# A token block on one core: tokens turned in groups of four tiles, and the modulation sums spread over the head steps

## The chip, the cores and the metric

The program runs on one core of one Trainium2 chip. The metric is the device time of one execution in microseconds (us); three runs are summed up by their median. On a core, TensorE (PE) multiplies matrices, VectorE (DVE), ScalarE (ACT) and GpSimd (POOL) work elementwise, and SyncE (SP) issues the transfers. Each engine works through its own list in order; they meet only at semaphores. Matrix products land in eight banks of 512 columns (PSUM), everything else is in SBUF.

## The reference

One layer of a diffusion backbone over 1024 latent tokens and 256 context tokens of width 1024. Six modulation rows (shift, scale and gate of two sub-layers) come from a SiLU of the condition times a 1024x6144 matrix. Rows 0 and 1 shape the input of the token mixer; row 2 gates its output; rows 3 and 4 shape the input of the feed-forward, row 5 gates that.

```python
def modulate(x, gain, shift, scale):
    return rms_norm(x, gain) * (1 + scale) + shift
...
        mx = jnp.split((sc @ w_mod[l] + b_mod[l])[:, None, :], N_MOD, axis=-1)
        px = split_proj(modulate(x, pre_mix_g[l], mx[0], mx[1]) @ w_in[l])
        pc = split_proj(modulate(xc, pre_mix_g[l], mc[0], mc[1]) @ w_in[l])
        oc, s_f, s_b = hgrn_bidir(*hgrn_inputs(pc, lb_f, lb_b), zero_state, zero_state)
        ox, _, _ = hgrn_bidir(*hgrn_inputs(px, lb_f, lb_b), s_f, s_b)
        mix_x = mixer_output(ox, px, rows, w_out[l], hgrn_onorm_g[l], conv_dw_w[l],
                             conv_dw_b[l], conv_ln_g[l], conv_ln_b[l])
        x = x + mx[2] * rms_norm(mix_x, post_mix_g[l])
        hx = swiglu(modulate(x, pre_ffn_g[l], mx[3], mx[4]), ffn_w_gate[l], ffn_w_up[l], ffn_w_down[l])
        x = x + mx[5] * rms_norm(hx, post_ffn_g[l])
```

The token mixer has four heads. Each head has seven projections (`b` and `a` for the convolution, `ff` and `fb` for the two forget gates, `q`, `g`, `v`), a two-way gated recurrence, and a convolution with 31 taps on 128 channels.

## The kernel before

**Front.** SP loads row 1 of the modulation matrix (eight tiles `mraw`), two token tiles with two weight tiles, then row 0, and then the other tokens. TensorE multiplies the rows by the condition (`mod_step`), ScalarE copies the product (`mod_rows`) and TensorE turns it into columns; VectorE adds the bias (`mod_take`). The ten token tiles (eight latent, then two of context) go one by one: ScalarE sums squares (`x_rms`), VectorE scales the tile (`norm_x`), TensorE transposes it in eight blocks (`turn_x`, line 618), VectorE applies gain and shift to each 128 columns (line 1387), ScalarE rounds to a high part (line 947), and GpSimd subtracts for the low part (`lo_part`, line 1238). Every large product is made of three products of such parts, so a tile can be used only once both parts stand.

**Head steps.** Step 0 runs the first head's projections. Steps 1 to 3 are one loop: each runs the projections of a head and between them the recurrence of the head before. A step has 20 units (`UNITS`): unit 0 and 1 `b`, 2 and 3 `a`, 4 to 6 `ff`, 7 to 9 `fb`, 10 and 11 `q`, 12 and 13 `g`, 14, 15 and 17 `v`; 16, 18 and 19 turn `v`. `PE_STEPS` fixes which uses of the recurrence follow a unit: the levels 0 to 7 after units 0 to 7, state products after 9 to 11, the output ("o") after 12, which needs the states of `rec_states`. Three banks turn over for units, five for uses. VectorE's order is `dve_body`: per unit `take`, `rec_step`, and as many convolution taps as `TAPS_AFTER` says. `rec_start` (lines 1433 to 1443) opens a step, before anything else.

**The other four rows.** Rows 2 to 5 of the modulation matrix are summed on VectorE in step 0, 32 chunks of 128x1024 (`mod_chunk`, lines 1369 and 1372) into four rows of `macc`. After step 0, TensorE sums them over partitions (`mod_sum`, 8 products each against a column of ones), VectorE takes them (`mod_take`, line 1350), and the loop waits for all four.

**Weights.** Three slots (`ringa`, `ringb`, `ringc`) hold weight tiles; tile p+1 of a slot is loaded when the last unit of the tile before it is done, ScalarE copies the high part (`head_hi`, line 935), GpSimd makes the low one. SP's queue is in order, so a load behind a waiting one waits too.

## Time and profile before

| | us |
|---|---|
| median of 3 runs | 1452.11 (1450.2 to 1452.63) |
| the profiled execution | 1452.88 |
| its span, first to last instruction | 1451.1 |
| TensorE busy | 1375.9 (95%) |
| VectorE, ScalarE, GpSimd busy | 778.6, 377.3, 324.2 |
| mean granted TensorE clock | 0.970 |

A row of the timeline gives start, duration, engine, line, operation and names, and in brackets how long the engine stood idle before, and what released it. A product of two 32-bit operands is two rows for TensorE, so "x16" of such a kind is eight products. A matmul's shown end is modelled and overlaps the next one by about 0.17 us.

### The profile page before, as it was taken

The numbers are of one execution on the slowest core, as the hardware profiler recorded it, in microseconds if no ns is written. First come the engines' busy times: TensorE is split into PE (matmuls) and PEld (weight loads), VectorE is DVE, ScalarE is ACT, GpSimd is POOL, SyncE is SP. The second block draws the span as 40 slices with busy tenths as digits, with TensorE's granted clock in tenths as the row PEclk, the third lists the DMA queues.
The fourth block names the chain that finished last, engine by engine and source line by source line (L and its number), as shares of the span: only waits on it lengthen the run. The fifth ranks groups of instructions, "written<-read, shape, count | busy, mean of one in ns | idle before, by whom it ended". The sixth has DMA issues, their size and how long they took to land. (4 is left out here: it accounts for less than half of the span.)

```text
span 1451.1 us, 17647 instructions
## 1 busy us (share of the span) xinstructions
PE 1375.9 (95%) x6725; PEld 1148.5 (79%) x6725; DVE 778.6 (54%) x1020; ACT 377.3 (26%) x562; POOL 324.2 (22%) x135
## 2 busy tenths in 40 slices
PE   6699899999999997898989999999999999999998
PEld 1588788888888886687768888888888888888876
DVE  2899969769778879818721313232232313232227
ACT  3521222132232234616631121111111121111112
POOL 1522111021111124503524122122122122122110
PEclk9699799999999998999999999999999999999999
DMA  9384110110010010004321111101101111101132
GB/s 370 155 284 165 29 30 16 30 44 28 29 43 29 14 68 34 1 25 164 136 68 29 50 39 58 58 31 57 57 29 58 49 39 57 58 30 57 51 124 116
DMA packets 94704, 101.94 MB, mean 70 GB/s; under 512 B 3118, under 2 KB 77091, under 8 KB 94658
## 3 DMA queue, kind: packets, MB, share of 16 engines
q1 hardware_dynamic: 94658, 101.32, 20.5%
q8 instruction: 29, 0.48, 0.1%
q14 instruction: 17, 0.14, 0.0%
HBM read 92.92 MB, written 8.39 MB: 70 GB/s over the span
## 5 line engine op out<-in xcount | busy, mean ns | idle before, releaser
L1238 POOL TENSOR_TENSOR slot<-slotraw,slot 128x1024 fp32r<-128x1024 f32 x66 | 160.5, 2442 | 522.2 <-ACT slot L1174 313.8
L561 PE MATMUL bank<-h2Ta,slot 128*128 128x512 f32 x1056 | 247.5, 394 | 5.2 <-POOL slot L1238 4.9
L561 PE MATMUL bank<-slot,mid 128*128 128x512 f32 x1056 | 242.9, 391 | 1.8 <-POOL slot L1238 1.8
L561 PEld LDWEIGHTS bank<-h2Ta,slot 128*128 128x128 f32 x1056 | 200.4, 190 | 47.8 <-POOL slot L1238 5.3
L561 PEld LDWEIGHTS bank<-slot,mid 128*128 128x128 f32 x1056 | 199.3, 189 | 43.8 <-POOL slot L1238 2.2
L561 PE MATMUL bank<-cathi,slot 128*128 128x512 f32 x704 | 220.2, 389 | 0.0
L1419 DVE SCALAR_TENSOR_TENSOR cat<-conv_u,taps,cat 128x784 f32 (+29 forms) x120 | 150.6, 1255 | 12.6 <-DVE cat L1419 6.2
L561 PEld LDWEIGHTS bank<-cathi,slot 128*128 128x128 f32 x704 | 132.1, 188 | 27.7 <-issue 0.3
L561 PE MATMUL bank<-hT,ringb 128*128 128x512 f32 (+1 forms) x672 | 149.1, 378 | 0.4 <-DVE cat L1402 0.4
L1694 DVE TENSOR_TENSOR mid<-bank,sgm 128x512 f32<-128x512 f32 x44 | 30.4, 692 | 221.7 <-ACT sgm L1189 221.7
L1719 DVE TENSOR_TENSOR arena<-bank,arena 128x512 f32<-128x512 f32 x144 | 99.5, 691 | 90.0 <-PE bank L561 89.5
L561 PE MATMUL bank<-catlo,slot 128*128 128x512 f32 x352 | 136.9, 389 | 0.0
L561 PEld LDWEIGHTS bank<-hT,ringb 128*128 128x128 f32 x672 | 118.6, 188 | 22.4 <-DVE cat L1402 0.8
L1697 DVE TENSOR_TENSOR mid<-bank,mid 128x512 f32<-128x512 f32 x44 | 30.4, 692 | 170.6 <-PE bank L561 170.5
L561 PE MATMUL bank<-hT,ringa 128*128 128x512 f32 (+1 forms) x480 | 109.1, 386 | 7.5 <-DVE mod L1350 5.5
L561 PEld LDWEIGHTS bank<-hT,ringa 128*128 128x128 f32 x480 | 87.0, 198 | 24.1 <-issue 5.5
L561 PE MATMUL bank<-hT,ringc 128*128 128x512 f32 (+1 forms) x480 | 102.8, 371 | 0.0
L561 PEld LDWEIGHTS bank<-hT,ringc 128*128 128x128 f32 x480 | 83.0, 189 | 14.3
L561 PE MATMUL bank<-wo,cathi 128*128 128x512 f32 x256 | 83.3, 407 | 5.3 <-POOL catlo L1238 3.7
L1189 ACT ACTIVATE sgm<-bank 128x512 f32<-128x512 f32 x44 | 26.1, 595 | 234.8 <-PE bank L561 234.8
L561 PEld LDWEIGHTS bank<-catlo,slot 128*128 128x128 f32 x352 | 66.1, 188 | 13.7
L561 PE MATMUL bank<-Q,KC 128*128 128x128 f32 x448 | 62.7, 297 | 10.1 <-DVE Q L1474 7.0
(171 smaller groups left out, 1516.7 us busy)
## 6 DMA issues: line engine op xcount, KB each, us to landing
mraw<-in_w_mod SPq DMA_DIRECT2D x48, 512.0 KB, 7.0
slotraw<-in_ffn_w_gate SPq DMA_DIRECT2D x22, 512.0 KB, 3.7
slotraw<-in_ffn_w_up SPq DMA_DIRECT2D x22, 512.0 KB, 3.8
slotraw<-in_ffn_w_down SPq DMA_DIRECT2D x22, 512.0 KB, 3.9
ringinb<-in_w_in SPq DMA_DIRECT2D x12, 512.0 KB, 3.6
xst<-in_x SPq DMA_DIRECT2D x8, 512.0 KB, 13.7
ringina<-in_w_in SPq DMA_DIRECT2D x8, 512.0 KB, 4.7
ringinc<-in_w_in SPq DMA_DIRECT2D x8, 512.0 KB, 4.7
```

What stands on the lines that cost most here:

```text
L561: return pe.matmul(o, l, r, start=start, stop=stop, skip_group_check=True)
L1189: act.activation(sgm[:, p, :], bank[gu_at(n, pos)[2]][:], ACT.Sigmoid).then_inc(gu_sig, 1)
L1238: return pool.tensor_tensor(lo, full, hi.bitcast(F32), ALU.subtract)
L1419: conv_last[0] = step(dve.scalar_tensor_tensor(out, src, w, out, ALU.mult, ALU.add))
L1694: dve.tensor_tensor(mid32[:, p, :], bank[b0][:], sgm[:, p, :], ALU.mult).then_inc(gu_part, 1)
L1697: dve.tensor_tensor(mid32[:, p, :], bank[b0 + 1][:], mid32[:, p, :], ALU.mult).then_inc(gu_free, 1)
L1719: ins = dve.tensor_tensor(y_half(t, hf), b[:], y_half(t, hf), ALU.add)
```

## The change

Four things are changed together.

First, tokens are turned in three groups (four latent tiles, four latent tiles, two context tiles). Instead of scaling a tile and transposing it, VectorE scales the identity (`diag`), and TensorE multiplies each 128x128 block of tokens by that diagonal, so that a block comes out turned and normalised; four tiles fill one bank, and one affine step covers 512 columns (256 for the context). ScalarE makes the high part straight from the bank (`part_hi`), VectorE the full one (`part_full`), and low parts alternate between VectorE (`part_lo`) and GpSimd. Five of the 24 turns stand between the fourth and the fifth chunk of the second modulation row.

Second, the second and third unit change places: unit 1 is now the first half of `a`, unit 2 the second half of `b`. Step 0 runs units 0 and 1 after group 0 alone.

Third, step 0 sums only rows 2 and 3 (16 chunks). Rows 4 and 5 are summed in the second and third steps, those with s = 1 and s = 2, in eight chunks each (`late_chunk`) through one buffer. The column sums (`mod_sum`) stand after unit 13 of step 0 (row 2) and ahead of unit 19 of steps 0, 1 and 2 (rows 3, 4, 5); VectorE takes each at the start of the next step (`late_take`), and unit 1 waits for it.

Fourth, the loop runs over s = 1 and 2, and step 3 is written out behind it.

```diff
...
+GROUPS = [range(0, 4), range(4, 8), range(8, 10)]
+XBANK = [0, 1, 2, 4, 6, 3, 5, 7] + [3 + r % 5 for r in range(16)]
...
+UNITS[1], UNITS[2] = UNITS[2], UNITS[1]
...
-CHUNKS_AFTER = [4, 4, 4, 4, 4, 4, 4, 4]
-TAPS_FIRST = [0, 0, 0, 0, 0, 0, 0, 0, 3, 3, 3, 3, 3, 3, 2, 2, 2, 2, 2, 2]
+CHUNKS_FIRST = [0, 2, 2, 2, 2, 2, 2, 2, 2]
+CHUNK_LATE = [3, 5, 7, 9, 11, 13, 15, 17]
+TAPS_FIRST = [0, 0, 0, 1, 1, 1, 1, 1, 1, 3, 3, 3, 3, 2, 2, 2, 2, 2, 2, 0]
...
+        macc = sb("macc", [P, DM], offset=spot["K"])
         vT = sb("vT", [P, 2, BANK], offset=RAW0 + RAW * 2 * DM * 4)
+        diag = sb("diag", [P, 8, P], offset=RAW0 + RAW * 2 * DM * 4)
...
+        def x_part(i):
+            g, k = i // KT, i % KT
+            t0, n = TORD[GROUPS[g][0]] * P, len(GROUPS[g]) * P
+            a = 1 if g == 2 else 0
+            return (slice(t0, t0 + n), bank[XBANK[i]][:, 0:n], xfull[:, i % 4, 0:n],
+                    gain[:, k, a:a + 1], mod[:, 0, k, a:a + 1])
...
+            def load_late(s, k):
+                sp.wait_ge(mod_used, s * KT + (KT + k))
+                sp.dma_start(mraw[:, 7, :].rearrange("p (o n) -> p o n", o=1),
...
             load_mod(0)
-            for t in range(2):
+            for t in range(4):
                 load_x(t)
-                load_tile(0, t)
+            load_tile(0, 0)
             load_mod(1)
...
+            load_tile(0, 1)
+            for t in range(4, NT):
...
             load_tile(0, 2)
-            for c in range(4 * KT):
-                if c in (12, 18, 24):
-                    load_tile(0, c // 6 + 1)
+            for c in range(2 * KT):
+                if c in (10, 12):
+                    load_tile(0, c // 2 - 2)
                 load_chunk(c)
+            load_tile(0, 5)
+            load_tile(1, 0)
             load_tile(0, 6)
-            with sp.Fori(1, HEADS) as s:
-                for p in range(NTILE):
-                    load_tile(s, p)
+            with sp.Fori(1, HEADS - 1) as s:
+                load_tile(s, 1)
+                load_tile(s, 2)
+                load_late(s, 0)
+                load_tile(s, 3)
+                load_tile(s, 4)
+                load_late(s, 1)
+                load_tile(s, 5)
+                for k in range(2, 5):
+                    load_late(s, k)
+                load_tile(s, 6)
+                load_tile(s + 1, 0)
+                for k in range(5, KT):
+                    load_late(s, k)
+            for p in range(1, NTILE):
+                load_tile(HEADS - 1, p)
...
+            def mod_sum(s, src, out):
+                pe.wait_ge(mod_used, s * KT + 2 * KT)
                 for j in range(KT):
-                    ins = mm(bank[LBASE + n - 2][:, j:j + 1], macc[:, n - 2, j * P:(j + 1) * P], ones[:, 0:1], True, True)
+                    ins = mm(out[:, j:j + 1], src[:, j * P:(j + 1) * P], ones[:, 0:1], True, True)
                 ins.then_inc(mod_turned, 1)
...
+            def turn_x(i):
+                g, k = i // KT, i % KT
+                if k == 0:
+                    pe.wait_ge(xn_ready, GROUPS[g][-1] + 1)
+                if i == 5:
+                    pe.wait_ge(mod_done, 2)
+                earlier = [j for j in range(i) if XBANK[j] == XBANK[i]]
+                if earlier:
+                    pe.wait_ge(x_hi, earlier[-1] + 1)
+                    pe.wait_ge(x_full, earlier[-1] + 1)
+                for c, t in enumerate(GROUPS[g]):
+                    ins = mm(bank[XBANK[i]][:, c * P:(c + 1) * P], xst[:, t, k * P:(k + 1) * P], diag[:, t % 8, :],
+                             True, True)
+                ins.then_inc(xp_full, 1)
...
+            for k in range(KT + 1):
+                mod_step(1, k)
+                if k == 3:
+                    for i in range(5):
+                        turn_x(i)
...
+                if u == NUNIT - 1 and row:
+                    mod_sum(s, cat[:, 3], b[:, 2 * P:])
...
+                        if first(s) and u in (0, 2, 4):
+                            i = u // 2 * KT + k
+                            pe.wait_ge(lo_pool if i % 2 else lo_dve, i // 2 + 1)
...
+            for i in range(5, KT):
+                turn_x(i)
             project(0, 0)
-            for t in range(7, NT):
-                turn_x(t)
-            for u in range(1, NUNIT):
-                if u == 1 or u == 4:
-                    pe.wait_ge(h_lo, 8 if u == 1 else NT)
+            project(0, 1)
+            for i in range(KT, 3 * KT):
+                turn_x(i)
+            for u in range(2, NUNIT):
                 project(0, u)
...
+                if u == 13:
+                    mod_sum(-1, macc[:], bank[LBASE])
...
+            def pe_step(s, row):
                 for u in range(NUNIT):
-                    project(s, u)
+                    if u == (NUNIT - 1) % GRING:
+                        pe.wait_ge(mod_done, s + 3)
+                    project(s, u, row)
                     for i in PE_STEPS[u]:
                         use(s - 1, i)
+            pe.wait_ge(mod_done, 3)
+            with pe.Fori(1, HEADS - 1) as s:
+                pe_step(s, True)
+            pe_step(HEADS - 1, False)
...
+            def part_hi(i):
+                sl, src, _, scale, shift = x_part(i)
+                act.wait_ge(mod_done, 2)
+                act.wait_ge(xp_full, i + 1)
+                act.activation(hT[:, 0, i % KT, sl], src, ACT.Identity, scale=scale, bias=shift).then_inc(x_hi, 1)
...
+            for t in range(4):
                 x_rms(t)
...
+            head_hi(0, 0)
...
+            for i in range(KT):
+                part_hi(i)
+            for t in range(4, 8):
+                if t == 5:
+                    head_hi(0, 1)
+                x_rms(t)
+            for i in range(KT, 2 * KT):
+                part_hi(i)
+                if i % KT in (3, 5):
+                    x_rms(7 + i % KT // 2)
+            for i in range(2 * KT, 3 * KT):
+                part_hi(i)
...
+            for g in range(3):
+                if g < 2:
+                    head_lo(0, g)
+                for i in range(g * KT + 1, (g + 1) * KT, 2):
+                    sl, _, full, _, _ = x_part(i)
+                    pool.wait_ge(x_full, i + 1)
+                    lo_part(hT[:, 1, i % KT, sl], full, hT[:, 0, i % KT, sl]).then_inc(lo_pool, 1)
...
-                dve.tensor_scalar(xst[:, t, :], xst[:, t, :], rr[:, 0, t:t + 1], None, ALU.mult).then_inc(xn_ready, 1)
+                if t >= 8:
+                    dve.wait_ge(xp_full, KT)
+                dve.tensor_scalar(diag[:, t % 8, :], ident[:], rr[:, 0, t:t + 1], None, ALU.mult).then_inc(xn_ready, 1)
...
+            def late_take(s):
+                dve.wait_ge(mod_turned, s + 3)
+                dve.wait_ge(gemm_act, s * N_GACT + N_GACT)
+                b = bank[(NUNIT - 1) % GRING][:, 2 * P:2 * P + KT]
+                dve.tensor_tensor(mod[:, bass.ds(s + 2, 1), :, 0:1], b.rearrange("p (o k a) -> p o k a", o=1, a=1),
+                                  vec[:, bass.ds(s * KT + (R_BM + 2 * KT), KT)].rearrange("p (o k a) -> p o k a", o=1, a=1),
+                                  ALU.add).then_inc(mod_done, 1)
...
+            def late_gains():
+                dve.wait_ge(mod_done, 6)
+                step(dve.scalar_tensor_tensor(gain2[:], mod[:, 4, :, 0], 1.0, vec[:, R_PREF:R_PREF + KT], ALU.add, ALU.mult))
+                step(dve.tensor_tensor(gate[:, 1], mod[:, 5, :, 0], vec[:, R_POSTF:R_POSTF + KT], ALU.mult))
+            def late_chunk(s, k):
+                dve.wait_ge(late_in, s * (16 * KT) + 16 * (k + 1 - KT))
+                src, w, acc = mraw[:, 7, :], silc[:, k, 0:1], cat[:, 3]
+                if k == 0:
+                    ins = dve.tensor_scalar(acc, src, w, None, ALU.mult)
+                else:
+                    dve.wait_ge(mod_used, s * KT + (KT + k))
+                    ins = dve.scalar_tensor_tensor(acc, src, w, acc, ALU.mult, ALU.add)
+                ins.then_inc(mod_used, 1)
...
-                src, w, acc = mraw[:, CHUNK_AT[c % NCH], :], silc[:, k, 0:1], macc[:, n, :]
+                src, w, acc = mraw[:, CHUNK_AT[c % NCH], :], silc[:, k, 0:1], cat[:, 3] if n else macc[:]
...
+            def part_full(i):
+                _, src, full, scale, shift = x_part(i)
+                dve.wait_ge(x_hi, i + 1)
+                if i >= 4 and i % 2:
+                    dve.wait_ge(lo_pool, (i - 4) // 2 + 1)
+                elif i >= 4:
+                    dve.wait_ge(lo_dve, (i - 4) // 2 + 1)
+                dve.tensor_scalar(full, src, scale, shift, ALU.mult, ALU.add).then_inc(x_full, 1)
+            def part_lo(i):
+                sl, _, full, _, _ = x_part(i)
+                dve.wait_ge(x_full, i + 1)
+                dve.tensor_tensor(hT[:, 1, i % KT, sl], full, hT[:, 0, i % KT, sl].bitcast(F32),
+                                  ALU.subtract).then_inc(lo_dve, 1)
...
+            for t in GROUPS[0]:
+                norm_x(t)
             mod_take(1)
...
+            for g in range(3):
+                if g:
+                    for t in GROUPS[g]:
+                        norm_x(t)
+                for i in range(g * KT, (g + 1) * KT, 2):
+                    part_full(i)
+                    part_full(i + 1)
+                    part_lo(i)
...
                     if rec:
                         rec_step(s - 1, u, 1)
+                        if u == 0:
+                            late_take(s)
+                        if more and u in CHUNK_LATE:
+                            late_chunk(s, CHUNK_LATE.index(u))
                     else:
-                        for c in taps_after(CHUNKS_AFTER, u):
+                        for c in taps_after(CHUNKS_FIRST, u):
                             mod_chunk(c)
+                        if u == 15:
+                            mod_take(2)
...
+            dve_body(HEADS - 1, True, TAPS_AFTER, False)
...
-                if u == 1:
+                if u == 0:
+                    late_gains()
...
```

On TensorE at the front, what stands from the first modulation row to the fifth unit, before:

```order
L561 MATMUL bank<-mraw,silc 32x512 x16
L561 MATMUL bank<-sel,mrow 128x2 x8
L561 MATMUL bank<-mraw,silc 32x512 x16
L561 MATMUL bank<-sel,mrow 128x2 x8
L618 MATMUL bank<-ident,xst 128x128 x56
L561 MATMUL bank<-hT,ringa 128x512 x24
L618 MATMUL bank<-ident,xst 128x128 x24
L561 MATMUL bank<-hT,ringa 128x512 x24
L561 MATMUL bank<-hT,ringb 128x512 x48
```

And in the changed program:

```order
L597 MATMUL bank<-mraw,silc 32x512 x8
L597 MATMUL bank<-diag,xst 128x128 x20
L597 MATMUL bank<-mraw,silc 32x512 x8
L597 MATMUL bank<-sel,mrow 128x2 x8
L597 MATMUL bank<-diag,xst 128x128 x12
L597 MATMUL bank<-hT,ringa 128x512 x24
L597 MATMUL bank<-hT,ringb 128x512 x24
L597 MATMUL bank<-diag,xst 128x128 x48
L597 MATMUL bank<-hT,ringa 128x512 x24
L597 MATMUL bank<-hT,ringb 128x512 x24
```

The turns now stand in three pieces (20 between the row's chunks, 12 ahead of unit 0, 48 behind unit 1), and two units run before the last 48.

On VectorE, the last taps of the loop's body before (`cat<-conv_u` is a tap; ISA and REGISTER_ALU rows are the sequencer's own):

```order
L1419 SCALAR_TENSOR_TENSOR cat<-conv_u,taps,cat 128x16x50
L359 REGISTER_ALU
L1419 ISA
L1419 SCALAR_TENSOR_TENSOR cat<-conv_u,taps,cat 128x16x49
L359 REGISTER_ALU
L1572 REGISTER_ALU
L1572 COMPARE_AND_BRANCH
```

And in the changed program, where `mraw` rows are late chunks:

```order
L1521 SCALAR_TENSOR_TENSOR cat<-conv_u,taps,cat 128x16x50
L1445 REGISTER_ALU
L1450 REGISTER_ALU
L1451 SCALAR_TENSOR_TENSOR cat<-mraw,silc,cat 128x1024
L365 REGISTER_ALU
L1521 ISA
L1521 SCALAR_TENSOR_TENSOR cat<-conv_u,taps,cat 128x16x49
L1450 REGISTER_ALU
L1451 SCALAR_TENSOR_TENSOR cat<-mraw,silc,cat 128x1024
L365 REGISTER_ALU
L1678 REGISTER_ALU
L1678 COMPARE_AND_BRANCH
```

The seventh and the eighth late chunk have one tap between them, and nothing behind them but the loop's branch.

On SP, the end of the loop's body before, the loads of the last two tiles:

```order
L468 DMA ringinc<-in_w_in 128x8x128
L465 REGISTER_ALU
L468 ISA
L468 DMA ringinb<-in_w_in 128x8x128
L484 REGISTER_ALU
```

And in the changed program:

```order
L482 DMA ringinb<-in_w_in 128x8x128
L481 ISA
L482 ISA
L482 DMA ringina<-in_w_in 128x8x128
L487 REGISTER_ALU
L488 ISA
L488 DMA mraw<-in_w_mod 128x1024
L487 REGISTER_ALU
L488 ISA
L488 DMA mraw<-in_w_mod 128x1024
L487 REGISTER_ALU
L488 ISA
```

The next step's first weight tile is now asked for in this body, and the last late chunks behind it; the next step's second tile comes behind these.

## Rows read from the trace of the kernel before

**Rows 1.** The page: busy time, share and instructions of each engine.

```profile
PE 1375.9 (95%) x6725; PEld 1148.5 (79%) x6725; DVE 778.6 (54%) x1020; ACT 377.3 (26%) x562; POOL 324.2 (22%) x135
```

**Rows 2.** Windows: us; busy (count) PE PEld DVE ACT POOL; granted clock, DMA share, GB/s.

```profile
45.00:56.00 11.00, 6.67 (x30) 5.47 (x29) 10.89 (x34) 7.94 (x14) 7.82 (x4) 0.50 0.46 189
63.00:66.00 3.00, 2.74 (x21) 2.29 (x19) 1.53 (x5) 0.20 (x1) 1.32 (x1) 1.00 0.00 0
```

**Rows 3.** TensorE's waits in 38 to 72 and 152 to 190: total, times, longest.

```profile
PE bank L618 <- DVE xst L1339: 10.1, 6, 2.3
...
PE bank L561 <- DVE mod L1350: 5.5, 1, 5.5
```

**Rows 4.** Timeline, the second modulation row: start, us, engine, line, names.

```profile
24.10 7.30 PE L561 MATMUL bank<-mraw,silc 128*32 128x512 f32 x24 [3.05 <-DMA mraw<-in_w_mod]
...
32.87 1.05 PE L561 MATMUL bank<-mraw,silc 128*32 128x512 f32 x4 [0.20 <-DMA mraw<-in_w_mod]
...
36.60 0.17 DVE L1347 TENSOR_TENSOR mod<-bank,vec 128x16 f32<-128x16 f32 x1 [8.74 <-PE bank L561]
```

**Rows 5.** Timeline, one token tile and the two units of 56 and 70.

```profile
54.69 2.64 DVE L1387 TENSOR_SCALAR xfull<-bank,gain,mod 128x128 f32<-128x128 f32 x8
...
56.45 7.54 PE L561 MATMUL bank<-hT,ringa 128*128 128x512 f32 x24
...
70.68 7.30 PE L561 MATMUL bank<-hT,ringa 128*128 128x512 f32 x24 [1.56 <-POOL hT L1238]
...
77.82 11.04 PE L561 MATMUL bank<-hT,ringb 128*128 128x512 f32 x48
78.02 0.60 ACT L968 ACTIVATE cat<-bank 128x512 f32<-128x512 f32 x1 [1.63 <-PE bank L561]
```

**Rows 6.** Timeline, the end of step 0 and the start of step 1.

```profile
144.04 5.79 PE L561 MATMUL bank<-hT,ringb 128*128 128x512 f32 x24 [0.42 <-DVE cat L1402]
...
153.96 11.99 PE L561 MATMUL bank<-ones,macc 128*128 128x1 f32 x64
...
171.40 8.09 PE L561 MATMUL bank<-hT,ringa 128*128 128x512 f32 x24 [5.45 <-DVE mod L1350]
171.49 1.80 DVE L1433 TENSOR_SCALAR K<-F,lb 128x1280 f32<-128x1280 f32 x2 [0.23 <-issue]
...
178.85 1.49 DVE L1443 TENSOR_TENSOR T<-F 128x1280 f32<-128x1280 f32 x1
...
179.33 3.73 PE L561 MATMUL bank<-qraw,K 128*128 128x128 f32 x32
```

**Rows 7.** Timeline of VectorE and GpSimd inside step 1; TensorE's waits for the states.

```profile
213.01 2.40 POOL L1238 TENSOR_TENSOR ringa<-ringina,ringa 128x1024 fp32r<-128x1024 f32 x1 [17.17 <-ACT ringa L935]
...
213.09 3.48 DVE L1474 TENSOR_TENSOR Q<-Q,T 128x512 f32<-128x512 f32 x2 [0.40 <-PE bank L561]
...
232.26 3.38 DVE L1474 TENSOR_TENSOR Q<-Q,T 128x512 f32<-128x512 f32 x2 [1.13 <-PE bank L561]
...
264.65 0.49 PE L561 MATMUL bank<-AT,V 128*128 128x128 f32 x2 [1.71 <-DVE S L1506]
```

**Rows 8.** Timeline, the end of step 1 and the start of step 2.

```profile
275.59 1.84 PE L561 MATMUL bank<-ones,AT 128*128 128x1 f32 x16
277.29 5.75 PE L561 MATMUL bank<-hT,ringb 128*128 128x512 f32 x24
...
285.94 4.67 DVE L1419 SCALAR_TENSOR_TENSOR cat<-conv_u,taps,cat 128x832 f32 x4
```

**Rows 9.** Timeline of TensorE: equal products behind two of its waits.

```profile
555.20 3.70 PE L561 MATMUL bank<-Q,KC 128*128 128x128 f32 x16 [4.87 <-DVE Q L1474]
588.36 2.78 PE L561 MATMUL bank<-Q,KC 128*128 128x128 f32 x16 [2.44 <-ACT KC L987]
```

**Rows 10.** The tile mraw: chunk adds, min/median/max ns; loads to landing.

```profile
L1372 DVE SCALAR_TENSOR_TENSOR macc<-mraw,silc,macc x28: 1279/1284/3299, 74.7 to 124.3; 128x1024 f32<-128x1024 f32 x28
...
DMA to landing us min/median/max: 3.5/7.0/11.6
```

More of the change, by code:

```diff
@@ L105 @@
     PE_STEPS[_at].append(_i)
-CHUNKS_AFTER = [4, 4, 4, 4, 4, 4, 4, 4]
-TAPS_FIRST = [0, 0, 0, 0, 0, 0, 0, 0, 3, 3, 3, 3, 3, 3, 2, 2, 2, 2, 2, 2]
+CHUNKS_FIRST = [0, 2, 2, 2, 2, 2, 2, 2, 2]
+CHUNK_LATE = [3, 5, 7, 9, 11, 13, 15, 17]
+TAPS_FIRST = [0, 0, 0, 1, 1, 1, 1, 1, 1, 3, 3, 3, 3, 2, 2, 2, 2, 2, 2, 0]
 TAPS_AFTER = [0, 0, 0, 0, 1, 1, 1, 1, 3, 2, 4, 4, 3, 3, 3, 3, 0, 1, 0, 0]
 assert sum(TAPS_FIRST) == sum(TAPS_AFTER) == TAPS - 1
-assert sum(CHUNKS_AFTER) == 4 * KT
+assert sum(CHUNKS_FIRST) == 2 * KT and len(CHUNK_LATE) == KT
 WO_ORDER = [0, 1, 2, 4, 5, 6, 7, 3]
@@ L398, in kernel_program @@
         MODS = [1, 0, 2, 3, 4, 5]
-        CHUNK_AT = [1, 2, 3, 5, 6, 7]
+        CHUNK_AT = [1, 2, 5, 6, 7]
         NCH = len(CHUNK_AT)
@@ L626, in wait_bank, with project @@
                 pe.wait_ge(act_sem if who == "act" else dve_sem, s * n + ((1 - ago) * n + k + 1))
-            def project(s, u):
+            def project(s, u, row=True):
                 p, kind, n = UNITS[u]
@@ L1349, in mod_take @@
                 else:
-                    dve.tensor_tensor(mod[:, m, :, 0], bank[LBASE + n - 2][:, 0:KT],
+                    dve.tensor_tensor(mod[:, m, :, 0], bank[LBASE][:, 0:KT],
                                       vec[:, R_BM + m * KT:R_BM + (m + 1) * KT], ALU.add).then_inc(mod_done, 1)
                 dve.wait_ge(mod_done, n + 1)
-                one = mod[:, m, :, 0]
                 if m == 1:
@@ L1356, in mod_take @@
                                                   ALU.add, ALU.mult))
-                elif m == 4:
-                    step(dve.scalar_tensor_tensor(gain2[:], one, 1.0, vec[:, R_PREF:R_PREF + KT], ALU.add, ALU.mult))
-                elif m in (2, 5):
-                    g, r0 = (0, R_POSTM) if m == 2 else (1, R_POSTF)
-                    step(dve.tensor_tensor(gate[:, g], one, vec[:, r0:r0 + KT], ALU.mult))
+                elif m == 2:
+                    step(dve.tensor_tensor(gate[:, 0], mod[:, m, :, 0], vec[:, R_POSTM:R_POSTM + KT], ALU.mult))
+            def late_take(s):
[18 more added lines that the diff above has]
+                ins.then_inc(mod_used, 1)
             def mod_chunk(c):
@@ L1373, in mod_chunk @@
                 ins.then_inc(mod_used, 1)
-            norm_x(0)
-            norm_x(1)
+            def part_full(i):
[11 more added lines that the diff above has]
+                                  ALU.subtract).then_inc(lo_dve, 1)
             mod_take(0)
+            for t in GROUPS[0]:
+                norm_x(t)
             mod_take(1)
             step.wait()
-            for t in range(NT):
-                a = 1 if TORD[t] < CT else 0
-                for k in range(KT):
-                    if k % 4 == 0:
-                        dve.wait_ge(xp_full, 2 * t + k // 4 + 1)
-                    if k == 0 and t >= 2:
-                        dve.wait_ge(h_lo, t - 1)
-                    ins = dve.tensor_scalar(xfull[:, t % 2, k, :],
-                                            bank[LBASE + (2 * t + k // 4) % 4][:, (k % 4) * P:(k % 4 + 1) * P],
-                                            gain[:, k, a:a + 1], mod[:, 0, k, a:a + 1], ALU.mult, ALU.add)
-                    if k % 4 == 3:
-                        ins.then_inc(xp_free, 1)
-                if t + 2 < NT:
-                    norm_x(t + 2)
+            for g in range(3):
[6 more added lines that the diff above has]
+                    part_lo(i)
             def take(s, u):
@@ L1548, in rec_step, with dve_body @@
                     rec_out(h, u)
-            def dve_body(s, rec, taps):
+            def dve_body(s, rec, taps, more):
                 for u in range(NUNIT):
```

64 lines of the change are left out of this document (14 added, 50 removed).

## The prediction

> **What bounds the kernel now.** I read the busy times first. TensorE works 1375.9 of 1451.1 us [rows 1], so a change pays only where it takes products away or an idle stretch of TensorE. Next I read TensorE's waits by releaser, and two stretches stand out. While tokens are turned it waits six times for VectorE to scale a tile, 10.1 us in all; before step 1 it waits once, 5.5 us, for the modulation rows [rows 3]. The timeline of the first stretch shows VectorE as the pacemaker: a tile's eight affine steps take 2.64 us [rows 5], the scaling comes on top, and TensorE runs at a granted clock of 0.50 [rows 2], its half level. At the end of step 0 the 64 rows of column sums run 11.99 us from 153.96, then comes the wait, then step 1 starts at 171.40 with a slow unit [rows 6]. Last I read the waits inside the loop, since work moves there: short ones, such as 1.71 us ahead of the output products [rows 7].
>
> The profiled execution is 1452.88: the span 1451.1 and 1.78 around it. It stands 0.77 above the median of 1452.11, so what I forecast for the profile is lowered by 0.7 or so. A measurement can't tell less than 0.2%, 2.9 us: "same" is 1449.2 to 1455.0.
>
> **Term 1, the front.** Row 0 of the modulation is complete at 36.77 (36.60 and 0.17) [rows 4]. Its eight chunks arrive in order, 32.87 - 24.10 = 8.77 over seven, 1.25 each [rows 4]. Two more token tiles and one weight tile less stand ahead of it on SP: one tile net, +1.25. Between its fourth and fifth chunk come 20 turn products. No row shows a product with a diagonal; by form the nearest are the column sums, 16 rows or eight products in 1.70 (277.29 - 275.59), 0.2125 each at the full clock [rows 8], and 32 products in 11.99, 0.375 each at the half [rows 6]. The 20 cost 4.25 or 7.5; I take 4.25, as they stand in a dense stretch. The last four chunks lie in memory by then and cost 0.53 to 1.05 each instead of 1.25. So M, both rows done, moves from 36.77 to about 40.4 (bounds 39.5 and 43.7).
>
> From M on VectorE makes group 0. No row shows an affine step of 512 columns from a bank; eight of 128 take 2.64 [rows 5], and one 1024-wide add 1.28 [rows 10]. I take 0.7 for 512 columns and as much for the subtraction: a pair of blocks is two affine steps and one low part, 2.05, and four pairs 8.2. With ScalarE's first high part (0.60 for 512 columns, [rows 5]) and GpSimd's last low part (half of 2.40 [rows 7], 1.2) unit 0 ends at about M + 10.5. Unit 1 wants its own weight tile, whose high part ScalarE makes behind eight activations, the table load and a sum of squares, and GpSimd the low one in 2.4: it starts near M + 12.2 and ends at M + 17.8. Then come group 1's 32 turns (6.8), VectorE's second 8.2 and the diagonals, group 2's 16 turns (3.4 to 5.1), and unit 2 starts at about M + 35.3 = 75.7. In the kernel before unit 1 starts at 70.68 [rows 5].
>
> **Term 2, the rest of step 0.** From 70.68 to the end of the last turned block, 153.96 + 0.15, are 83.43 us; unit 1 itself takes 7.14 of them (77.82 - 70.68) [rows 5, 6]. Left are 76.3, and two column sums of 1.70 are added: 79.7. Step 1 then starts at 155.4 to 155.8, against 171.40: 15.8 earlier. The gap of half-clock sums and waiting also goes, and with it the slow unit behind it: 179.33 - 171.40 = 7.93 against about 5.56 for a unit at the full clock (5.75 with the overlap, [rows 8]), 2.4. Term 2 with term 1 is -18.2. Both ends: -21 if VectorE's affine steps are at 0.6 and the tail of group 2 hides, -14 if the 20 turns go at the half clock and VectorE pays for every pair separately. What was the column sums' cover before, 16 chunks on VectorE beside step 0, goes to the loop.
>
> **Term 3, unit 1 of step 1.** It now waits for `late_take`, which stands behind `rec_start` and the first `rec_step` on VectorE. `rec_start` takes 8.85 us (171.49 to 178.85 and 1.49) [rows 6]. When it can begin depends on what VectorE has left of step 0. Behind unit 13, which ends near 144.04 [rows 6], 12 taps are left at 1.17 (4.67 for four, [rows 8]) and up to 1.28 each, 14 to 15.4, and TensorE has 10.1 + 1.7 + 1.7 of work to the end of the step: VectorE is about 1 us late. GpSimd's low parts hold it up too: two VectorE instructions of 512 columns took 3.48 beside a GpSimd row that began 0.08 earlier, where one of 1024 takes 1.28 [rows 7, 10]; I add one such 2.1. Step start + 12.1 against TensorE's arrival after unit 0 and level 0, 5.56 + 3.5 = 9.04: a wait of 3.1, and 0.7 of clock behind it, +3.8. Bounds 0 (VectorE on time, not blocked) and +6 (two blocks). Steps 2 and 3 have the same wait in their list, but there the taps end earlier, and I charge none.
>
> **Term 4, steps 1 and 2 with the late chunks.** Three costs each.
> The sum ahead of unit 19: 1.70 [rows 8].
> The output products: TensorE waits 1.71 for the states [rows 7]. Chunks after units 3, 5, 7, 9 stand ahead of that on VectorE: one of about 0.75 and three of 1.28 with some blocking, 4.8. The pauses of VectorE that can take it up are 0.40 and 1.13 and the like [rows 7], some 3.3 by then. Bounds of the growth 1.1 (a pause I haven't seen takes more) and 4.8 (none does); by the pauses 1.5 would come out, but they lie ahead of the third chunk for the most part, and I take 2.8.
> The last chunk: all eight go through one buffer, and chunk 7 is asked for when chunk 6 has been added, after unit 15. A load of `mraw` takes 3.5 us at least, 7.0 in the median [rows 10]; those were issued in crowds, one alone is nearer the 3.5. Add 1.28 for the chunk and one tap. Between unit 15's take and unit 19's sum TensorE has units 16 to 18 and three turned pieces, and VectorE reaches chunk 6 itself late, 15 slots down its list. I get a wait of 3.2; bounds 0 and 6.5 (the median landing).
> A clock that falls in these waits: behind a wait of 4.87 sixteen products took 3.70, behind 2.44 2.78 [rows 9], against about 1.87 (32 in 3.73, [rows 6]); behind a wait of 1.71 two ran in 0.49 at full pace [rows 7]. So a wait of 3 to 4 costs some 1.2 more in all (0 to 3).
> Together 1.70 + 2.8 + 3.2 + 1.2 = +8.9 for a step, +17.8 for both; bounds +5.6 and +32, of which the far one wants every wait at its worst.
>
> **Term 5, small things.** Step 3 is written out and its output wait may lose 1.71 [rows 7], as VectorE's list there is free of register instructions: -1.7 (bound 0). `late_gains`, two rows of 0.17 like the one in [rows 4], stand where TensorE waits 4.87 for VectorE [rows 9]: +0.35. Units 1 and 2 change places: the same 48 products; VectorE's work on them moves by one unit and was waited for by nobody: 0 (bounds -1 and +1).
>
> Sum: -18.2 + 3.8 + 17.8 - 1.7 + 0.35 = +2.05, 1454.9 for the profiled execution, 1454.2 for the median.
>
> **Rivals.**
> A, the forecast: what the front gives back the loop takes. Its own range is 1450.5 to 1458, from each wait moved by a third of its bounds.
> R1, slower: the load-to-add chain of the single buffer decides. If a load takes 5 us or more under the weights' traffic, chunks 5 to 7 slide and the sum of unit 19 waits 6.5 instead of 3.2, twice, and the clock falls behind it: 2 x 3.3 + 1 = +7.6, 1461.8. It decides from a landing of about 4.5 us on. For it: the median 7.0 [rows 10]. Against it: the transfers in the loop are few.
> R2, faster: VectorE has more slack than I see, being 54% busy [rows 1]. Then unit 1 of step 1 doesn't wait (-3.8) and the output wait doesn't grow by more than 1.1 (2 x -1.7): 1447.0. Against it: rows such as 3.48 instead of 1.28 beside GpSimd [rows 7], and that the waits for states are already there.
> R3, the clock in the front rises: now TensorE has products that are no transposes. Unit 0 then takes 5.75 and not 7.54 [rows 5, 8], and the last four chunks go at 0.53: -2.7, 1451.5. For it: 0.50 while transposes are waited for [rows 2]. Against it: 63 to 66 was at 1.00 with transposes running, though right behind a unit, and 45 to 56 had TensorE idle for 4 of 11 us, which explains the half level as well [rows 2].
> The Trainium skill, "TensorE: Matmul & The Clock Gate", section "Part 4: PE-mode transpose", states that the full clock doesn't engage for transposes, which don't count as busy in the same way. By that rule R3 is what would come; the trace doesn't settle it, since its fast transposes could have inherited the clock of the unit ahead of them.
> R4, slower: SP's queue is in order, and weight tiles now stand behind chunk loads: tile 3 of step 0 behind chunk 9, and the next step's tile 1 behind the eighth late chunk, which is asked for only after chunk 6 is added. If that is later than the slot came free, unit 2 of the next step starts on its weights late, by about 2.5 us twice: +5, 1459. Against it: tile 1 has the whole of unit 0 and unit 1, 15 us, before it is wanted.
>
> **How the numbers follow.** A 0.47, of which 0.04 is faster, 0.31 same, 0.12 slower by more than 0.2%; R1 0.21 (slower); R2 0.18 (faster); R3 0.09 (same); R4 0.05 (slower). Faster 0.22, same 0.40, slower 0.38. The time is A's, 1454.2. From 1447 to 1461 the range takes in A, R3, R4, half of R1 and more than half of R2; what is left out is under 2 in 10.
>
> **What would show it in the profile after.** M at 40.4 and the 20 turns at 0.2125 each; unit 0's end at 51, unit 1 at full speed, unit 2 at 75.7; the granted clock of 30 to 60, which tells R3; step 1's start at 155.6; TensorE's wait for `late_take` before step 1's unit 1 (3.1, none in steps 2 and 3); the output waits of steps 1 and 2 (4.5, from 1.71) and of step 3 (0); the wait ahead of the sum before unit 19 (3.2) with the landing time of the late loads, which tells R1; and no wait of ScalarE's copy for the tile of unit 2, which tells R4. I am wrong if step 1 starts later than 159, if the sum's wait is near 0, or if TensorE shows no new wait in the loop.

## The result and the profile after

The changed kernel takes 1460.87 us (1459.87 to 1461.79) against 1451.87: ratio 1.0063, 95% interval 1.0046 to 1.0081. It is slower by 9.0 us where 1454.2 was forecast, at the far edge of the stated range (1447 to 1461). The profiled execution is 1461.46, its span 1459.7.

The timeline of TensorE up to unit 2, and between its rows VectorE's take of the second modulation row (start, us, engine, line, names):

```profile
30.84 4.88 PE L597 MATMUL bank<-diag,xst 128*128 128x128 f32 x40
...
40.31 0.17 DVE L1416 TENSOR_TENSOR mod<-bank,vec 128x16 f32<-128x16 f32 x1 [13.85 <-PE bank L597]
...
53.20 5.73 PE L597 MATMUL bank<-hT,ringb 128*128 128x512 f32 x24 [1.34 <-POOL ringb L1304]
...
71.93 5.56 PE L597 MATMUL bank<-diag,xst 128*128 128x128 f32 x32 [5.84 <-DVE diag L1408]
...
77.24 3.02 PE L597 MATMUL bank<-hT,ringa 128*128 128x512 f32 x12
```

M, the time at which both modulation rows are done, is 40.48 (forecast 40.4), unit 1 starts at 53.20 (52.6), unit 2 at 77.24 (75.7). In the kernel before, two units and all turns were done by 77.82 [rows 5], here by 77.24: turning in groups is worth 0.6 us by then, although VectorE no longer paces each tile. One wait of 5.84 for the last diagonals took the place of most of the six (10.1 in all).

The end of step 0, and TensorE's two long waits of step 1:

```profile
155.92 5.74 PE L597 MATMUL bank<-hT,ringa 128*128 128x512 f32 x24
161.50 3.73 PE L597 MATMUL bank<-qraw,K 128*128 128x128 f32 x32
167.75 7.31 PE L597 MATMUL bank<-hT,ringb 128*128 128x512 f32 x24 [2.52 <-DVE mod L1433]
...
253.45 0.80 PE L597 MATMUL bank<-AT,V 128*128 128x128 f32 x2 [3.32 <-DVE S L1608]
...
287.21 3.58 PE L597 MATMUL bank<-ones,cat 128*128 128x1 f32 x16 [2.95 <-DVE cat L1451]
290.65 0.67 PE L688 MATMUL bank<-ident,vT 128*128 128x128 f32 x2
290.97 7.13 PE L597 MATMUL bank<-hT,ringa 128*128 128x512 f32 x24
```

Step 1 starts at 155.92 instead of 171.40 [rows 6]: 15.5 us are won. Then they are lost. Behind each wait the reader sees products that should be faster: sixteen column-sum rows in 3.58 that take 1.84 elsewhere [rows 8], a first unit in 7.13 instead of 5.73. The windows around them (us; busy of PE, PEld, DVE, ACT, POOL; granted clock, DMA share, GB/s) show why:

```profile
253.00:257.00 4.00, 3.55 (x19) 3.55 (x20) 3.51 (x6) 0.00 (x0) 0.00 (x0) 0.57 0.19 35
257.00:260.00 3.00, 3.00 (x29) 3.00 (x28) 2.30 (x2) 0.00 (x0) 0.00 (x0) 1.00 0.33 128
...
287.00:291.00 4.00, 3.79 (x19) 3.79 (x19) 0.28 (x2) 0.00 (x0) 0.00 (x0) 0.52 0.92 300
```

Behind these waits of about 3 us TensorE runs at its half level (1.2 GHz): for some 3 us behind the waits for the states (253.4 to 256.5) and for nearly 7 behind those ahead of the sum (287.2 to 294.0). From level 0 to level 0 (the products of `qraw` and `K`) step 1 is 136.44 us long and step 2 132.76, where the kernel before has 121.00 and 120.97.

VectorE at the end of step 1:

```profile
280.58 1.28 DVE L1451 SCALAR_TENSOR_TENSOR cat<-mraw,silc,cat 128x1024 f32<-128x1024 f32 x1
281.78 1.03 DVE L1521 SCALAR_TENSOR_TENSOR cat<-conv_u,taps,cat 128x784 f32 x1
285.88 1.28 DVE L1451 SCALAR_TENSOR_TENSOR cat<-mraw,silc,cat 128x1024 f32<-128x1024 f32 x1 [3.07 <-DMA mraw<-in_w_mod]
290.88 1.80 DVE L1535 TENSOR_SCALAR K<-F,lb 128x1280 f32<-128x1280 f32 x2 [3.72 <-issue]
```

The last chunk waits for its load, which is asked for at 282.0, when the chunk before it is added, and lands 3.7 later. Then come 3.72 us in which VectorE waits for nothing that the profile shows. They lie at the loop's jump back: in the trace VectorE's row of the branch (line 1678) ends at 286.21, and its next row of any kind, at the head of the loop, begins at 290.60. Before step 3, which follows without a jump, rec_start begins at 419.81, right behind the chunk of 418.60 to 419.88.

The tail lost 1.1 us:

```profile
552.45 2.31 DVE L1440 SCALAR_TENSOR_TENSOR gain<-mod,vec 128x8 f32<-128x8 f32 x1
...
558.34 5.58 DVE L1576 TENSOR_TENSOR Q<-Q,F 128x512 f32<-128x512 f32 x2
...
564.06 3.49 PE L597 MATMUL bank<-Q,KC 128*128 128x128 f32 x16 [6.27 <-DVE Q L1576]
```

The wait of [rows 9] grew from 4.87 to 6.27. An instruction of `late_gains` that writes eight numbers per partition took 2.31 us beside GpSimd's low parts, not 0.17; but the next ones took longer too (the two of `Q` 5.58, in the kernel before 4.62). Whether the wait hangs on `late_gains`, 'take first' tells.

### The profile page after: what moved, and what is told of

Read it like the earlier page. It is cut to its first block and busy times, and to the rows that moved or that the text cites. A ratio compares the mean times of both kernels' runs of the same rounds, so it can differ in the third digit from the quotient of the medians.

```text
span 1459.7 us, 17675 instructions
## 1 busy us (share of the span) xinstructions
PE 1379.7 (95%) x6805; PEld 1156.9 (79%) x6805; DVE 763.3 (52%) x976; ACT 381.9 (26%) x576; POOL 318.5 (22%) x137
## 5 line engine op out<-in xcount | busy, mean ns | idle before, releaser
L1521 DVE SCALAR_TENSOR_TENSOR cat<-conv_u,taps,cat 128x784 f32<-128x784 f32 (+29 forms) x120 | 149.9, 1249 | 8.4 <-DVE cat L1521 4.1
L597 PE MATMUL bank<-Q,KC 128*128 128x128 f32 x448 | 62.5, 297 | 12.9 <-DVE Q L1576 8.6
```

The lines of the kernel that those rows point to most:

```text
L597: return pe.matmul(o, l, r, start=start, stop=stop, skip_group_check=True)
L1521: conv_last[0] = step(dve.scalar_tensor_tensor(out, src, w, out, ALU.mult, ALU.add))
```

## Experiments

Times are medians; the kernel before, run beside them, was 1451.1, 1451.5 and 1451.6.

**What the additions cost.** The loads and `late_chunk` are left out, so rows 4 and 5 are not summed; the column sums and takes stay.

```diff
...
-                        if more and u in CHUNK_LATE:
-                            late_chunk(s, CHUNK_LATE.index(u))
...
```

> Left out: the loads and the additions of modulation rows 4 and 5 (the column sums, the takes and all other instructions stay, on a row that is already there). Theory 'clock': the waits ahead of unit 19 and their slow products go (12.1), and ahead of the output products 2 x 1.6 of waiting and 2 x 1.42 of slow products: 1460.9 - 18.1 = 1442.8. Rival 'the loop costs for another reason' (units changed in order, the written-out third step, the sums themselves): it stays above 1452. The two column sums of 1.70 are in either number.

1441.50, ratio 0.9935 (0.9921 to 0.9948). The wait for the states is back to 1.69 with no slow product behind it, and the sum runs without a wait:

```profile
251.07 0.49 PE L591 MATMUL bank<-AT,V 128*128 128x128 f32 x2 [1.69 <-DVE S L1602]
...
280.30 1.84 PE L591 MATMUL bank<-ones,cat 128*128 128x1 f32 x16
```

So 19.4 us hang on sixteen additions and their loads. The additions take about as long on VectorE (14 of 1.28 and two of 0.73), an engine that is busy for half the time. The rival falls: neither the changed order of units nor the sums themselves cost them.

**The clock apart from the waits.**

```diff
...
+                    if not first(s):
+                        fill(b[:, 3 * P:4 * P], 14, P)
                     mod_sum(s, cat[:, 3], b[:, 2 * P:])
...
```

and the same (14 spare products) ahead of the wait for the states.

> In steps 1 and 2 TensorE runs 14 spare products of 128 columns (about 3.0 us) ahead of the column sum's wait, and 14 ahead of the wait for the states; nothing reads them. The waits' length is filled, not removed. Theory 'clock': the granted clock stays up, and only the slow products behind the waits go: 1.74 + 1.40 + 1.43 + 1.74 ahead of and behind the step's end, 2 x 1.42 at the output products, 9.1 in all, so 1451.8. Rival 'waits alone': 1460.9, or 1 more where the filler overshoots.

1458.80, 2.1 less than the changed kernel, not 9.1. The two steps tell different things. Step 2, level 0 to level 0, is 127.38 instead of 132.76: 5.4 less for waits that are about as long as before, only full of spare products. The granted clock of 419 to 427 is 1.00. Of the 5.4, 0.45 is unit 1's wait for the take, which is gone too; the rest agrees with the 4.8 of slow products counted in that step. So there the clock accounts for some four tenths of the 11.8 us that the step had grown by. In step 1 a stall of TensorE at the jump took the gain:

```profile
286.19 1.84 PE L597 MATMUL bank<-ones,cat 128*128 128x1 f32 x16
287.90 0.41 PE L694 MATMUL bank<-ident,vT 128*128 128x128 f32 x2
292.27 7.33 PE L597 MATMUL bank<-hT,ringa 128*128 128x512 f32 x24 [3.96 <-issue]
```

TensorE's row of the branch lasts 5.65 us here and 0.23 in the changed kernel, and the unit behind the stall is slow again.

**The sum's place.**

```diff
...
-                if u == NUNIT - 1 and row:
-                    mod_sum(s, cat[:, 3], b[:, 2 * P:])
...
+                    if u == 0:
+                        pe.wait_ge(gemm_act, s * N_GACT + N_GACT)
+                        mod_sum(s - 1, cat[:, 3], bank[(NUNIT - 1) % GRING][:, 2 * P:])
```

> The column sums of rows 3, 4 and 5 stand behind unit 0 of the next step instead of ahead of unit 19; all else as in the changed kernel (1460.9). Theory 'clock': each of the two waits ahead of unit 19 (2.95 and 2.86 us) costs its own length and, by a granted clock that falls in it, slow products behind it (the sum 3.58 and 3.27 instead of 1.84, the first unit of the next step 6.97 and 7.31 to its successor instead of 5.57). Both go: 2.95 + 2.86 + 1.74 + 1.43 + 1.40 + 1.74 = 12.1, so 1448.8. Rival 'waits alone' (the slow products are slow for a reason of their own, such as one-column products): only 5.8 goes, 1455.1, and the first units of steps 2 and 3 stay near 7.1. Rival 'the wait moves': the last chunk is late at the new place too, 1457 or more.

1457.89 (1455.35 to 1460.64), ratio 1.0045. The first units of steps 2 and 3 are fast again (5.72), so the slow products are not slow of themselves. But the time is that of the rival 'the wait moves':

```profile
293.85 3.84 PE L597 MATMUL bank<-qraw,K 128*128 128x128 f32 x32 [0.96 <-DVE K L1536]
301.15 5.72 PE L597 MATMUL bank<-hT,ringb 128*128 128x512 f32 x24 [3.46 <-DVE mod L1434]
```

Unit 1 of step 2 starts at 301.15, only 1.0 earlier than in the changed kernel (302.12). A second chain ends there: last chunk, VectorE's stall of 4.08 at the jump, rec_start, take. TensorE's wait and its slow products in front had run beside it. In step 3, with no jump, unit 1 is 4.5 earlier (429.68 against 434.19).

The row at 301.15 shows something else: its unit stands behind a wait of 3.46 and still takes 5.72, at a granted clock of 1.00 from 301 to 307. The length of a wait alone doesn't decide whether the clock falls behind it.

**The take, and the gains of the tail.** `late_take` stands ahead of rec_start, `late_gains` after the last swish.

> VectorE takes each late row before rec_start instead of behind it, and late_gains stands where VectorE is idle in the tail. Theory 'clock': in step 1 the wait of unit 1 (2.52) and the slow unit behind it (7.15 instead of 5.55 to its successor, 1.6) go, in step 2 0.45, and in the tail VectorE's rows before the products no longer contain the 2.31 of late_gains, 1.1: 1460.9 - 5.7 = 1455.2. Rival 'waits alone': 1456.8. Rival 'VectorE is late with rec_start anyway': level 0 or 1 waits instead, 1460.

1454.39, ratio 1.0013 (1.0004 to 1.0022): 6.5 less, where 5.7 was expected. Unit 1 of step 1 starts at 165.76, with no wait, and takes 5.70. But 1.1 of the 5.7 was to come from the tail, and it didn't; step 2 gave 2.3 instead of 0.45. There the products behind the wait for the states, as long as in step 1 (3.31 and 3.34), kept the full clock, and the output took 5.38 instead of 7.01. The windows behind the wait in step 1 and in step 2:

```profile
250.00:254.00 4.00, 4.00 (x22) 4.00 (x23) 3.75 (x4) 0.00 (x0) 0.00 (x0) 0.58 0.32 92
382.00:387.00 5.00, 5.00 (x45) 5.00 (x46) 4.49 (x5) 0.00 (x0) 0.00 (x0) 1.00 0.34 105
```

So part of the good agreement is luck. The tail's wait stays at 6.2 without `late_gains` in front, so the 2.31 was not its cause:

```profile
548.90 3.65 DVE L1568 TENSOR_TENSOR K<-K,F 128x1280 f32<-128x1280 f32 x1 [2.23 <-ACT KC L1052]
552.47 5.58 DVE L1576 TENSOR_TENSOR Q<-Q,F 128x512 f32<-128x512 f32 x2
```

VectorE now idles 2.23 for ScalarE where it was blocked before, and the products with `Q` are as slow beside GpSimd. How these lists meet GpSimd's decides the wait (4.0 in 'all moved', 6.2 here, 5.9 to 6.2 in the changed kernels written out, 3.9 in the kernel before written out), and no run here sorts it out.

**The chunks' places**, on top of the moved sum.

```diff
...
-CHUNK_LATE = [3, 5, 7, 9, 11, 13, 15, 17]
+CHUNK_LATE = [0, 1, 2, 11, 12, 13, 14, 15]
...
```

> As 'sum behind unit 0' (1457.9, its profiled execution 1456.0), and the eight late chunks stand after units 0, 1, 2, 11, 12, 13, 14, 15 instead of 3, 5, ..., 17, with the loads moved ahead on SP to match. Theory 'VectorE's list sets both ends' (the chunks ahead of the states; at the step's end the last chunk behind its load, then 4.08 us at the loop's branch, then rec_start, then the take): the output waits fall from 3.3 to about 1.7 and their slow products (1.42) go, twice, 6.0; and with the last chunk over before unit 16, the wait of unit 1 in steps 2 and 3 (3.46 and 0.6) goes for the most part, 3: 1457.9 - 9 = 1449. Rival 'the chunks only move their cost' (VectorE's early pauses are not there, and levels 1 to 3 wait instead): 1456 to 1460.

1449.55, ratio 0.9984 (0.9976 to 0.9993). The two waits for the states are 3.4 together instead of 6.6; three chunks at the start of a step fit into pauses in which VectorE waited for TensorE. The time is the expected 1449, but the waits at the start of steps 2 and 3 did not go for the most part: level 0 waits 2.57, unit 1 1.83 and 1.93. The jump costs more here: 5.93 us lie between VectorE's row of the branch and its next row, although the last chunk is over before.

**All of it**: the moved sum, the chunks' places, the take in the middle of rec_start, the gains.

> As 'early_chunks', and the take of a late row stands in the middle of rec_start (ahead of its products with Q), and late_gains stands where VectorE is idle in the tail. Theory: on top of 'early_chunks' step 1's wait of 2.5 and its slow unit (1.6) go, and 1.1 in the tail: 1449 - 5.2 = 1444, faster than the kernel before (1451.1). Rival 'a waiting take in rec_start delays level 0 or 1': 1448.

1439.29, ratio 0.9927 (0.9912 to 0.9943): faster than both kernels, and 4.7 under what was expected. Of these, 2.3 are the tail's wait, 3.95 instead of 6.26. What is left at the start of step 2 is the stall at the jump, 5.23 here, and again slow products (5.18 instead of 3.82) behind a short wait:

```profile
284.66 1.80 DVE L1536 TENSOR_SCALAR K<-F,lb 128x1280 f32<-128x1280 f32 x2 [5.23 <-issue]
...
286.51 5.18 PE L597 MATMUL bank<-qraw,K 128*128 128x128 f32 x32 [1.33 <-DVE K L1536]
```

**The loop's own cost.** Five kernels have the steps written out on TensorE, VectorE, ScalarE and SyncE (the kernel before on TensorE, VectorE and SyncE alone):

```diff
...
-            with dve.Fori(1, HEADS - 1) as s:
+            for s in range(1, HEADS - 1):
...
```

> As 'sum behind unit 0' (1457.9), with steps 1 and 2 written out on TensorE, VectorE, ScalarE and SyncE instead of a loop. Theory 'branch': VectorE's 4.08 us of idling between the last chunk and rec_start is the jump back; without it rec_start of step 2 starts near 287.5 and unit 1's wait of 3.46 falls to about 0.3: 1454.5. Rival 'issue is something else' (fetching goes on at the same pace without a branch): 1457.9, with the same idle time.

1445.01 (1439.8 to 1452.8), ratio 0.9963 (0.9950 to 0.9977): 12.9 less than its loop form, not 3.4. VectorE's row of rec_start follows the last chunk at once:

```profile
279.51 1.28 DVE L1452 SCALAR_TENSOR_TENSOR cat<-mraw,silc,cat 128x1024 f32<-128x1024 f32 x1 [2.63 <-DMA mraw<-in_w_mod]
280.71 1.80 DVE L1536 TENSOR_SCALAR K<-F,lb 128x1280 f32<-128x1280 f32 x2
```

> The changed kernel (1460.9) with steps 1 and 2 written out on TensorE, VectorE, ScalarE and SyncE. Theory 'the loop form itself burdens VectorE' (register instructions ahead of taps and chunks, and the 3.7 us before rec_start at the jump back): the waits for the states fall from 3.3 to about 1.9, twice, with less slow work behind them, and step 2's 0.45 goes; the waits ahead of unit 19 stay, since they hang on the load: 1460.9 - 5 = 1456. Rival 'only the jump': 1460.4. Rival 'the longer code costs fetches': over 1461.

1449.02, ratio 0.9989 (0.9979 to 0.9999): 11.9 less than the loop form, more than any of the three theories had. The rest is seen in VectorE's taps, loop form first, then written out:

```profile
357.69 1.10 DVE L1521 SCALAR_TENSOR_TENSOR cat<-conv_u,taps,cat 128x848 f32 x1
358.97 1.12 DVE L1521 SCALAR_TENSOR_TENSOR cat<-conv_u,taps,cat 128x864 f32 x1 [0.18 <-DVE cat L1521]
360.27 1.13 DVE L1521 SCALAR_TENSOR_TENSOR cat<-conv_u,taps,cat 128x880 f32 x1 [0.18 <-DVE cat L1521]
```

```profile
349.23 5.81 DVE L1521 SCALAR_TENSOR_TENSOR cat<-conv_u,taps,cat 128x848 f32<-128x848 f32 x5
```

In the loop form each tap behind a tap starts 0.15 to 0.19 late, twelve times a step (2.1 us), in front of the states and of the last chunk. The register instructions that stand between them there are the likely reason; no run takes them out alone. The waits for the states are 1.9 and 2.2 then, and those ahead of unit 19 1.8 and 1.9.

> As 'filled waits' (14 spare products ahead of each of the two long waits of steps 1 and 2), with the steps written out. In the loop form the filler saved 5.4 us in step 2, as the theory of the clock said, but in step 1 a stall of 3.96 at the jump back took the gain. Theory 'clock': without a jump the whole 9.1 comes: 9 less than 'changed unrolled', less what the shorter waits for the states there no longer cost, so 6 to 9 less. Rival 'waits alone': the same time as 'changed unrolled'.

1449.07, the same as 'changed unrolled': my expectation fell. The waits have shrunk to 1.8 to 2.2 and the filler takes 3.1, so it overshoots each by about 1.2, which eats what the clock gave. In 'changed unrolled' the output products behind a wait of 1.91 ran at full pace (5.35 for the whole), but behind the wait of 1.79 the sum took 2.23 and the unit after it 6.86, 1.5 more together:

```profile
281.09 2.23 PE L597 MATMUL bank<-ones,cat 128*128 128x1 f32 x16 [1.79 <-DVE cat L1451]
...
283.50 6.86 PE L597 MATMUL bank<-hT,ringa 128*128 128x512 f32 x24
```

This run's time says nothing for or against the clock; step 2 of 'filled waits' does.

> The kernel before (1451.5) with its steps 1 to 3 written out on the same engines. It tells what of the gain of 'sum behind unit 0, unrolled' (12.9 us against its loop form) is the loop's own cost and has nothing to do with the late rows. Theory 'the loop form costs only where VectorE is short of time': VectorE has slack in this kernel (waits for states of 1.71, three times), so 3 x 1.7 at most and likely half: 1448 to 1451. Rival 'the loop form costs TensorE in each step': 1439 or so, 4 us a step.

1445.37, ratio 0.9958 (0.9944 to 0.9971): 6.2 less, between the theory (1448 to 1451) and its rival (1439). The three waits for the states, 5.1 together, are gone. So about half of what writing out gives the changed kernel, it gives the kernel before too. The other half goes with the late rows, which made VectorE late, and with the longer stall at the jump; no run parts the two.

> 'All moved' (1439.3) with steps 1 and 2 written out. There a wait of 1.33 for rec_start behind the jump, with 1.36 of slow products behind it, and two waits of 1.7 for the states are left. Theory: the first goes wholly, the others by half: 1439.3 - 4.4 = 1435. Rival 'written-out code has nothing left to give here': 1439.

1436.75, ratio 0.9900 (0.9885 to 0.9915), the fastest of all. As expected within 2 us: with the pauses already used well there is less for it to give.

**The clock in the front**, in the kernel before.

```diff
...
-                        ins = pe.transpose(bank[LBASE + n % 4][:, k * P:(k + 1) * P], xst[:, t, kk * P:(kk + 1) * P],
-                                           ident[:])
+                        ins = mm(bank[LBASE + n % 4][:, k * P:(k + 1) * P], xst[:, t, kk * P:(kk + 1) * P],
+                                 ident[:], True, True)
...
```

> The kernel before (1451.1), with its 80 turned blocks made by an ordinary product with the identity (two rows each) instead of a transpose. Rule of the Trainium skill, 'TensorE: Matmul & The Clock Gate', section 'Part 4: PE-mode transpose' (a transpose doesn't count as busy, so the full clock doesn't engage): the granted clock of 45 to 56 rises from 0.50 to 1.00 and unit 0 takes 5.75 instead of 7.54, 1449 or so. Rival 'the clock falls because TensorE is idle between the tiles': the clock of 45 to 56 stays at 0.50, unit 0 stays at 7.5, the time stays within 1 us, or the products at half clock and the waits for VectorE grow by a little, 1452.

```profile
45.00:56.00 11.00, 6.76 (x53) 6.19 (x54) 10.89 (x34) 7.94 (x14) 7.42 (x4) 1.00 0.50 204
```

```profile
55.40 2.05 PE L561 MATMUL bank<-ident,xst 128*128 128x128 f32 x16 [1.36 <-DVE xst L1339]
57.20 5.73 PE L561 MATMUL bank<-hT,ringa 128*128 128x512 f32 x24
...
75.64 4.70 PE L561 MATMUL bank<-hT,ringb 128*128 128x512 f32 x20
```

TensorE waits for VectorE as before and is busy for as long (6.76 of 11 us, 6.67 in [rows 2]), yet the clock is 1.00 instead of 0.50, and unit 0 takes 5.73 instead of 7.54. The Trainium skill ("TensorE: Matmul & The Clock Gate", "Part 4: PE-mode transpose") states that the full clock doesn't engage for transposes; these two windows agree, and my rival fell. The time stays, 1451.15 (ratio 1.0002): the 2.2 us won by 75.64 are lost at the end of step 0, in two waits for VectorE: 2.16 instead of 0.42 ahead of the unit at 143.61, and 6.66 instead of 5.45 for the last rows ahead of step 1.

## Why the prediction was wrong

Forecast for the profile was +2.05, measured is +8.6 (spans 1459.7 and 1451.1).
- **Term 1 and 2, right.** Step 1 starts 15.5 earlier (forecast 15.8), its first unit is fast, and its level 0 is 17.8 earlier (18.2).
- **R3** came: the clock of 45 to 56 is 1.00 in the changed kernel too. It gave little, as unit 0 waits for its low parts and unit 1 for its weights (1.34):

```profile
45.00:56.00 11.00, 9.27 (x37) 6.31 (x37) 8.88 (x15) 7.27 (x15) 7.36 (x4) 1.00 0.37 150
```

- **Term 3, right in sum,** by two errors that cancel. The wait of unit 1 is 2.52 (3.1), the slow unit behind it costs 1.6 (0.7): 4.1 against 3.8.
- **Term 4, waits near, clock wrong: this is the step that failed.** The output wait grew by 1.6 (2.8), the wait ahead of unit 19 is 2.95 and 2.86 (3.2), the load lands in 3.7. But "a wait of 3 to 4 costs some 1.2 more in all" was mis-sized. I priced by [rows 9] one piece of work behind one wait (its x16 rows are eight products, not sixteen) and took it for the sum. There are two waits in a step, and the slow clock goes on into the next work: 1.4 at the output products, 1.7 at the sum, 1.4 at the next unit; in step 2 1.6, 1.4 and 1.7. That is 4.6 and 4.8 instead of 1.2 each, 7.0 more than forecast. Against it stand waits that I had too long (2 x 1.2 at the output, 0.6 ahead of the sums). Small waits that I hadn't (0.37 and 0.22 ahead of state products, 0.45 for the take of step 2) and slow products beside them add some 1.4, so that term 4 is about 5.4 off. The rest of the 6.6 is 0.4 in the front, 0.3 in term 3, 0.8 in the tail and -0.2 in step 3. 'Filled waits' shows the clock's part in step 2, 5.4 less; for step 1 it is worked out from the durations alone, and 'sum behind unit 0' shows that part of it there lay beside VectorE's chain.
- **The signs.** None of my signs for being wrong came, as they asked for waits alone. I had named none for the products behind the waits.
- **A term was missing.** VectorE's stall at the jump, 3.72, was in no term: in the kernel before it is 0.84 at most at that place. In the changed kernel itself it runs beside TensorE's wait and slow products and shows only as the 0.45 of the take; but it keeps step 2's unit 1 from starting before 301 even when the sum is moved. Why it is long there and not in the kernel before stays open. The wait for the load isn't the reason: in 'no chunks' no load stands at the end of the body, and it is 3.34. The body is longer there (312 rows of VectorE in the trace, 286 in the kernel before), but in 'no chunks' it has only 290.
- **Term 5.** The output wait of step 3 is gone, -1.7 as forecast. The tail's wait grew by 1.4, not 0.35, and not by `late_gains`; 1.1 of it is left in the time.
- **R1** has the right size (1461.8) by a wrong way: the load isn't slow (3.7, the late loads 3.5 to 4.5), and the wait is 3, not 6.5.

## What to carry to other kernels

A wait of TensorE can cost more than its own length. Behind waits of 2.5 to 3.3 us the products took 1.4 to 3.2 us longer in all cases but one; so count the products that follow until the clock is back, over the borders of steps. Don't make a rule of the length: a wait of 1.33 cost 1.4 in 'all moved', waits of 3.46 and 3.31 cost nothing. Look at the granted clock behind each.

Work given to a half idle engine is free only in the pauses where it waits. The same sixteen additions cost 19.4 us in one set of places. In 'all moved' the kernel takes 1439.3, less than the one without the additions (1441.5), which still has the wait of 2.5 for the take and the longer one in the tail; so they are cheap there, though no run shows that they are free.

Look at a loop's jump back for idle time that is ended by nothing, and compare with a pass that has no jump behind it.

## What the runs showed of the hardware

- A jump back cost VectorE much in all seven loop forms of the changed kernel. From its row of the branch to its next row went 2.8 ('no chunks'), 4.4 to 4.8 (five of them, the changed kernel 4.39) and 5.9 us ('the chunks' places', where the profile puts the idle time down to ScalarE's copy of unit 0, for which rec_start doesn't wait). In the kernel before it was 0.3, and the last pass of the loop, which doesn't jump, shows 0.05 where no chunk is running. TensorE stalled for 3.96 in one form whose body was longer.
- The Trainium skill ("Runtime: NRT & Kernel Launch", "Instruction fetch mechanics") states that a taken branch whose target isn't at hand has to fetch it first. That would fit; written out, the idle time is gone. But the kernel before jumps back too, and pays 0.3, so no run here shows that it is the fetch.
- Transposes held the clock at 0.50 where ordinary products of the same blocks, with the same pauses between, had 1.00.
- Eight blocks turned by ordinary products took 2.05 us at the full clock, eight transposes 1.97 at the half level. Eight transposes in the stretch behind unit 0, with the clock at 1.00 (67 to 70), took 1.09.
